# Who makes the low parts of the weights: VectorE's subtraction, or ScalarE's negated copy and an accumulating DMA of GpSimd

## The reference

```python
h = rmsnorm(x, norm_pre_mix[layer]) * (1.0 + sc_m) + sh_m
proj = h @ w_in[layer]
(hq, hf, hi, hg, aq, ak, av, iq, ik, iw) = jnp.split(proj, split_points, axis=-1)
o_hg = hgrn2_mixer(hq, hf, hi, hg, lb_all[layer], hgrn_out_norm[layer])   # 4 heads, gated recurrence
o_att = dsa_mixer(aq, ak, av, iq, ik, iw, positions, ...)                 # 4 heads, top-128 keys of an indexer
y = jnp.concatenate([o_hg, o_att], axis=-1) @ w_out[layer]
x = x + gt_m * rmsnorm(y, norm_post_mix[layer])
```

## Time and profile before

| | us |
|---|---|
| median of 3 runs | 700.05 (699.14 to 700.44) |
| the profiled execution's own time | 701.65 |
| its span, first to last instruction | 699.9 |

### The profile page before, as it was taken

One profiled execution on the slowest core, in us unless ns is written; L12 is line 12 of the kernel. 1 busy time (PEld: TensorE's weight loads), 2 busy tenths in 40 slices (PEclk: granted clock), 3 DMA queues, 4 the chain that ended last, 5 costly groups with the idle time before them and its releaser, 6 DMA issues.

```text
span 699.9 us, 13262 instructions
## 1 busy us (share of the span) xinstructions
PE 684.1 (98%) x4712; PEld 572.6 (82%) x4712; DVE 579.1 (83%) x946; ACT 340.5 (49%) x581; POOL 161.1 (23%) x121
## 2 busy tenths in 40 slices
PE   8999999999999999999979999999999999999997
PEld 6566677777777787888659999999999998888885
DVE  4778999889898999988999999999999985344444
ACT  7367653545534344637744555555555561122123
POOL 4000000000000000000276576667666700000000
PEclk9999999999999999999989999999999999999999
DMA  9963223222224657478122553444344343332202
GB/s 280 357 198 86 61 62 83 68 90 60 62 62 124 226 162 273 147 245 237 30 92 63 149 146 111 133 134 129 116 131 120 98 144 121 100 110 90 61 5 115
DMA packets 97706, 88.90 MB, mean 127 GB/s; under 512 B 2735, under 2 KB 86787, under 8 KB 97670
## 3 DMA queue, kind: packets, MB, share of 16 engines
q1 hardware_dynamic: 97670, 88.44, 41.6%
HBM read 86.33 MB, written 2.10 MB: 126 GB/s over the span
## 4 chain that ended last, share of the span: by engine, by line
PE 61%; DVE 4%; issue 1%; ACT 1%; DVEq 0%; ACTq 0%
PE ps L2175 28%; PE ps L1672 17%; PE ps L1653 6%; PE ps L1690 6%; PE ps L2011 1%; PE ps L1991 1%; DVE w_lo L1017 1%; DVE h_hl L1131 1%; PE ps L2004 0%; DVE act L1125 0%; PE ps L1711 0%; DVE w_lo L1545 0%; ACT h_hl L586 0%; DVE act L1390 0%; DVE act L1108 0%
## 5 line engine op out<-in xcount | busy, mean ns | idle before, releaser
L1653 PE MATMUL ps<-h_hl,w_hi 128*128 128x512 f32 x480 | 158.9, 412 | 2.6 <-DVE w_lo L1017 2.6
L2175 PE MATMUL ps<-h_hl,w_hi 128*128 128x256 f32 x640 | 116.1, 283 | 0.0
L537 ACT ACTIVATE w_hi<-w_raw 128x1024 fp32r<-128x1024 f32 (+1 forms) x68 | 68.6, 1013 | 93.7 <-PE ps L1672 83.9
L1653 PEld LDWEIGHTS ps<-h_hl,w_hi 128*128 128x128 f32 x480 | 86.9, 191 | 25.5 <-issue 5.5
L2175 PEld LDWEIGHTS ps<-h_hl,w_hi 128*128 128x128 f32 x640 | 100.0, 192 | 0.2
L1653 PE MATMUL ps<-h_hl,w_lo 128*128 128x512 f32 x240 | 95.1, 396 | 0.0
L2175 PE MATMUL ps<-h_hl,w_lo 128*128 128x256 f32 x320 | 90.6, 283 | 0.0
L1672 PE MATMUL ps<-w_hi,ht_hl 128*128 128x512 f32 x288 | 88.8, 389 | 0.0
L2175 PE MATMUL ps<-ht_hl,w_hi 128*128 128x256 f32 x480 | 87.4, 283 | 0.6 <-ACT mix L941 0.6
L1017 DVE TENSOR_TENSOR w_lo<-w_raw,w_hi 128x1024 fp32r<-128x1024 f32 (+1 forms) x68 | 82.3, 1213 | 4.4 <-ACT w_hi L537 3.9
L2175 PEld LDWEIGHTS ps<-ht_hl,w_hi 128*128 128x128 f32 x480 | 74.9, 192 | 0.8 <-ACT mix L941 0.8
(11 more groups left out here) (310 smaller groups left out, 1300.9 us busy)
## 6 DMA issues: line engine op xcount, KB each, us to landing
w_raw<-in_w_ffn_in SPq DMA_DIRECT2D x44, 512.0 KB, 4.3
w_raw<-in_w_in SPq DMA_DIRECT2D x28, 512.0 KB, 4.0
w_raw<-in_w_ffn_out SPq DMA_DIRECT2D x22, 512.0 KB, 3.5
act<-in_w_ada SPq DMA_DIRECT2D x12, 512.0 KB, 8.1
adaw<-in_w_ada SPq DMA_DIRECT2D x6, 1024.0 KB, 5.2
act<-in_w_ada SPq DMA_DIRECT2D x6, 1024.0 KB, 5.2
res<-in_x SPq DMA_DIRECT2D x8, 512.0 KB, 5.6
w_raw<-in_w_out SPq DMA_DIRECT2D x8, 512.0 KB, 5.3
```

What stands on the lines that cost most here:

```text
L537: sc.activation(w_hi[slot][:, 0:n], w_raw[slot][:, 0:n], ACT.Copy).then_inc(hi_ok, 1)
L1653: last = mm(ps[bank][0:rows, :], a, b, start=(k == 0 and n == 0), stop=(k == KT - 1 and n == 2))
L2175: last_mm = mm(ps[bank][:, 0:HALF], a, b, start=(start and k == 0 and n == 0), stop=(k == 3 and n == 2), skip_group_check=not start)
```

## The change

For the 24 groups 12 to 35 (recurrent heads 1 to 3 and all of attention), the low part isn't written by DVE any more. ACT writes the negated rounded weights to w_lo and then the rounded weights to w_hi. GpSimd waits for that, issues a DMA that adds w_raw onto w_lo (float32 onto float32r, in place in SBUF), waits until it has landed, and raises lo_ok. On DVE the subtractions of these groups go, and the first one of the output projection (G_OUT) moves behind the rotation of the last attention head, with a wait for lo_ok of all groups before it. Two semaphores of loads (last_loaded and post_loaded) become one to make room for the two new ones.

```diff
@@ block.gpsimd
+            def add_low(g, n, slot):
+
+                pool.wait_ge(hi_ok, g + 1)
+                pool.sem_inc(pool_waits, 1)
+                pool.dma_start(w_lo[slot][:, :], w_raw[slot][:, :], accum_op=ALU.add).then_inc(low_added, 16)
+                pool.wait_ge(low_added, n * 16 + 16)
+                pool.sem_inc(lo_ok, 1)
+
+            pool.wait_ge(lo_ok, G_HG + 4)
+            with pool.Fori(1, HG_HEADS) as h:
+                for j in range(4):
+                    add_low(h * 4 + (G_HG + j), h * 4 + (j - 4), j)
+            with pool.Fori(0, ATT_HEADS) as h:
+                for j in range(3):
+                    add_low(h * 3 + (G_ATT + j), h * 3 + (4 * HG_HEADS - 4 + j), j)
             pool.wait_ge(att_out, ATT_HEADS)
@@ block.scalar
+            def split_both(slot, use, free):
+
+                sc.wait_ge(w_loaded[slot], use * 16 + 16)
+                sc.wait_ge(group_done, free)
+                sc.activation(w_lo[slot][:, :], w_raw[slot][:, :], ACT.Copy, scale=-1.0)
+                sc.activation(w_hi[slot][:, :], w_raw[slot][:, :], ACT.Copy).then_inc(hi_ok, 1)
...
-                split_hi(0, hh + (U_HG[0] + 1), hh * 4 + (G_HG + 1))
+                split_both(0, hh + (U_HG[0] + 1), hh * 4 + (G_HG + 1))
...
-                split_hi(1, hh + (U_HG[1] + 1), hh * 4 + (G_HG + 2))
+                split_both(1, hh + (U_HG[1] + 1), hh * 4 + (G_HG + 2))
...
                     if j == 0:
-                        split_hi(2, h + U_ATT[2], h * 3 + G_ATT)
+                        split_both(2, h + U_ATT[2], h * 3 + G_ATT)
                     else:
-                        split_hi(j - 1, h + (U_ATT[j - 1] + 1), h * 3 + (G_ATT + j))
+                        both = split_hi if isinstance(h, int) and h == ATT_HEADS - 1 else split_both
+                        both(j - 1, h + (U_ATT[j - 1] + 1), h * 3 + (G_ATT + j))
@@ block.vector
-                if isinstance(h, int) and h == 0:
-                    split_lo(G_HG + 4, 0)
...
-                    if isinstance(h, int) and h == HG_HEADS - 1:
-                        if st in (1, 4, 9):
-                            split_lo(*{1: (G_ATT + 1, 1), 4: (G_ATT + 2, 2), 9: (G_ATT + 3, 0)}[st])
-                    elif st in (1, 3, 6, 8):
-                        at, slot = {1: (5, 1), 3: (6, 2), 6: (7, 3), 8: (8, 0)}[st]
-                        split_lo(h * 4 + (G_HG + at), slot)
...
-                if not (first or last):
-                    split_lo(h * 3 + (G_ATT + 4), 1)
...
-                        split_lo(h * 3 + (G_ATT + 5), 2)
...
-                    split_lo(h * 3 + (G_ATT + 6), 0)
                     att_rotate(h + 1)
+                    if h == ATT_HEADS - 2:
+                        ve.wait_ge(lo_ok, G_OUT)
+                        split_lo(G_OUT, 0)
```

More of the change, by code:

```diff
@@ L193, in build @@
         gate_zero, gate_bias = sem("gate_zero"), sem("gate_bias")
-        last_loaded = sem("last_loaded")
         post_loaded, tail_loaded, tail_k = sem("post_loaded"), sem("tail_loaded"), sem("tail_k")
@@ L232, in build @@
         gate_sum, up_sum = sem("gate_sum"), sem("up_sum")
+        low_added, pool_waits = sem("low_added"), sem("pool_waits")
         silu_done, act_ok = [sem(f"silu_done{v}") for v in range(2)], [sem(f"act_ok{v}") for v in range(2)]
@@ L383, in _ @@
             sp.wait_ge(xs_ok, KT)
-            sp.dma_start(gate_ffn, norm_post_ffn.broadcast_to([P, D_MODEL])).then_inc(last_loaded, 16)
+            sp.dma_start(gate_ffn, norm_post_ffn.broadcast_to([P, D_MODEL])).then_inc(post_loaded, 16)
             sp.wait_ge(gate_zero, 2)
@@ L673, in hg_f @@
                 if not (isinstance(hh, int) and hh == 0):
-                    split_hi(2, hh + U_HG[2], hh * 4 + (G_HG - 1))
+                    split_both(2, hh + U_HG[2], hh * 4 + (G_HG - 1))
                 sc.wait_ge(group_done, hh * 4 + (G_HG + 1))
@@ L683, in hg_q @@
                 if not (isinstance(hh, int) and hh == 0):
-                    split_hi(3, hh + U_HG[3], hh * 4 + G_HG)
+                    split_both(3, hh + U_HG[3], hh * 4 + G_HG)
             def hg_i(hh):
@@ L1425, in att_body @@
                         normalise(t - 1)
-                    if first and t == 1:
-                        split_lo(G_ATT + 4, 1)
                     if last and t < 3:
@@ L1559, in scale_gate @@
             def scale_gate():
-                ve.wait_ge(last_loaded, 16)
+                ve.wait_ge(post_loaded, 32)
                 for b in range(2):
```

## The result

The changed kernel takes 737.15 us (median of 6, 735.42 to 738.89), the kernel before 700.25 (median of 6, 699.14 to 701.6). The ratio is 1.0526, 95% interval 1.0504 to 1.0549: 36.9 us slower. The forecast was 714, 13.95 us above the median then at hand. The direction held, and 737.15 lies just inside the stated range of 701.5 to 738; but the size was short by more than half. The profiled execution took 737.42 us, its span 735.7, against a span of 699.9 before.

What follows compares the result with a forecast made beforehand. PE's own work was taken as the bound. Waits of 12.2 us at L = 4.6, plus 3.9 contention, less 1.9 gain, made 14.2 us: 714 us against the median, range 701.5 to 738.

Steps and rivals of the forecast that it cites:

- The clock: PE after waits of 4 us and more: some 6.9 us at 1.2 GHz, losing 3.4 us; priced only in a rival.
- L: Time from the end of the w_hi copy to lo_ok; taken as 4.6 us, possible from 2.6 to 7.0.
- contention: Attention heads 1 to 3, slot 2, beside a 1 MB sum load: 1.3 us each, 3.9 us together.
- What bounds the kernel: 85 to 300 us: PE's own work bounds; busy 214.97 of 216 us over 88 to 304 us.
- The gain: DVE loses 24 subtractions; PE gains 0.85 us at the second attention head and 1.0 at four places: 1.9 us.
- the rival: ACT's second copy delays exp or level copies; PE waits 1 us in three attention heads, about 703 us; chance 0.03.
- The rooms: PE's first matmul of each group less split start plus 2.1 us: 1.4 to 4.6 at eleven groups, 13 others 5 or more.
- the store's 2.6: Within L: the 512 KB store out of SBUF, 2.6 us from issue to landing, taken as the nearest transfer.
- the second read: Within L: the add must also read its destination, charged at 1.7 us.
- long-add rival: Pool's DMA: engines add slowly or issue is slow; L at 6.5 us, about 737 us; chance 0.21.
- The cheap transfer: Pool's DMA: the add costs as little as a plain transfer; L at 3.3 us, about 700.6 us; chance 0.13.
- the signs named ahead: Landing 4 to 5 us; PE waits 3 us at head 1, 2 to 3 at attention's slot 2, less at slots 1, 3.

Runs made afterwards that it cites:

- small sum loads: The changed kernel with the twelve 1 MB loads of the running sums cut to an eighth of their bytes: 721.92 us, ratio 1.0323.
- moved split: The kernel before with slot 1's DVE subtraction of attention heads 1 and 2 moved behind the first two row maxima: 699.42 us, ratio 0.9998.

## Why the prediction was wrong in size and right in direction

Three terms of the sum failed. The clock stood in it at nothing, with no reason given, and cost 8.7 us net; L was taken as 4.6 us and is 5.2, which is 6.6 us over eleven groups; and contention was put at 3.9 us and is 8.5.

**What bounds the kernel** held: PE had no slack between 85 and 300 us, and each late low part went into the time.

**The gain** was put at 1.9 us; without the transfer it is 1.3. The part that the prediction read, what PE gets from DVE up to the end of attention, is 2.3 in the two profiles; the rest is the item below.

**ACT** was charged nothing. That holds for the 24 copies that were meant: without the transfer PE waits for none of them. It misses the negated copy for group 37, which the prediction didn't see in the code and which costs 0.6 to 0.8 us. As the bound, the way the rival had it (703 us, PE waiting for L823 or L714), ACT is out: 698.55.

**The rooms** held. With L = 5.2 they give the recurrent part 3.8 + 2 x 1.7 + 1.4 + 3 x 1.1 + 0.6 = 12.5 us. The waits are 3.73, then 2.23 and 1.64, then 1.40, then 0.84, 0.85 and 0.52, and none at the last: 11.2. For attention without large sum loads they give 2.1 each, with 1.83, 1.93 and 1.99 measured. That waits add up held too (14.9 + 23.4 against 36.9).

**L was mis-sized**, 4.6 against 5.2 quiet. By its terms: the store's 2.6 stood for a plain copy of 2.9; the second read was charged 1.7 and costs 1.6; GpSimd's own part was 0.3 and is 0.57 before the issue and 0.1 behind the landing. At the eleven groups with rooms of 4.6 or less the 0.6 us became 18.8 - 12.2 = 6.6 us of the sum. The Trainium skill, "DMA: Bandwidth & Descriptors", section "Anatomy of one DMA", gives an estimate of 3.2 us for such a transfer. The plain copy's 2.9 us (fastest) and 4.1 (median) lie around it; the add's 4.5 don't, so it is no price for an accumulating transfer.
The Trainium skill, "SBUF — State Buffer", section "Who interferes with whom", describes a lock between DVE and the descriptor writing of GpSimd. If it shows in the length of GpSimd's issues, it was small here: 24 of them took 859 ns in the median and 1255 at most, so at most 0.4 us once.

**Contention was mis-sized**: 3 x 1.3 = 3.9 us, with bounds of 0 and 2.5 each. Measured, attention's three waits are 13.97 us, 7.7 above what the rooms give for L = 5.2, or 2.6 each, just over the upper bound, and 0.85 at a fourth group. The failing step is taking half of the sum load's queue time: two large transfers in flight together end late both, and the sum loads too land in 7.1 and 8.1 us over 268 to 282 us, where the median before is 5.2.

**The clock was left out of the sum.** It stood in the long-add rival alone, tied to waits of 4 us and more. It fell after waits of 3.79, 3.73 and 2.23 us too. 11.4 us of cost less the 2.7 that the kernel before pays make 8.7.

Together: 14.2, + 6.6 for L, - 1.3 as the recurrent waits are a little under the rooms' value, + 4.6 for contention, + 8.7 for the clock, + 0.6 for the smaller gain, - 2.1 for PE's shorter waits at the feed-forward's start, + 2.3 lost again behind it: 33.6 us, against 35.8 between the two spans. Of the other 2.2, 1.8 are in how a wait is counted: the starts of PE's matmuls move by 27.8 us at the eleven waits, whose idle time is 26.0. The 2.3 us lost again don't look like the change's: the same loss stands, as 2.1 and 2.3, in the two other profiles with the short wait at the feed-forward's start (small sum loads, moved split), and are 0.7 at most in the rest. Why is open.

**The rivals.** The long add named 737 us, which is what came, but that is luck, for it came another way: it wanted L = 6.5 everywhere, and L is 5.2 in the quiet stretches and 7.1 to 8.9 in three groups. The cheap transfer gave 700.6 for an L of 3.3; a plain copy, at L = 3.6, took 715.9. That rival's error is the forecast's own: it too left out contention and clock. Of the signs named ahead, the landing of 4 to 5 us held only in quiet stretches, and the waits came where they were said to be, but up to twice as long.

## What to carry to other kernels

Where the bounding engine has no slack, write down each group's room and compare it with the whole handover: the engine's reaction, issue, landing in the busiest stretch of the queues, and the last signal. A transfer next to 1 MB loads should be priced at their common end, not at its quiet landing. Work moved off an engine that isn't the bound pays only at places with room (two of 24 groups gave 0.25%), and a stall of PE costs what it lasts plus half of the time that PE then works at 1.2 GHz, less what this hides. Look too for copies that the change makes where nothing needs them: one of them cost this kernel 0.6 us of its gain.

## What the runs showed of the hardware

- GpSimd begins to issue 0.57 us after the end of the copy that it waits for; the issue takes 0.86 us for an accumulating transfer of 512 KB inside SBUF and 0.53 us for a plain one.
- The add costs 1.6 us over a plain copy of the same 512 KB (4.5 against 2.9 us to landing); half of the columns take 3.2 us.
- Beside loads of 1 MB the same transfer takes up to 11.3 us to land, and the loads themselves 7.1 to 8.1 us in that stretch; with these loads cut to an eighth it takes 6.2 at most.
- In the changed kernel the granted clock fell to 1.2 GHz for 3.4 or 6.9 us at PE's waits of 2.23, 3.73, 3.79, 4.81 and 5.37 us, and at no shorter one; it began between 1.4 us before the wait's end and 1.0 us behind it. Over all runs the length of a wait doesn't decide alone: with small sum loads it fell behind one of 1.83 us; with the add started early it didn't behind one of 2.82, and with half of the add not behind one of 3.63. With the wait of 4.8 us filled by transposes it stayed at 2.4 GHz.
- At the start of the feed-forward part PE's wait for DVE has one of two values over the twelve profiled executions: 2.6 us (before, no transfer, and seven others) or 1.1 (after, small sum loads, moved split). The two groups don't go by what the kernels change; as each kernel has one profile, no run shows that one kernel has both.
